# Key pass of a decoder's attention: transposes and scores of two units at a time, with eight places for turned keys

## The reference, cut to what matters

```python
# selected branch, per sequence b and kv head g (4 kv heads of 4 query heads, head size 128)
kg = gather_paged_rows(pool_k, page_table, new_k, kpos)        # raw rows of a paged cache
s  = einsum('btgrd,btgkd->btgrk', q, kg) * ATTN_SCALE
p  = masked_softmax(s, mask)
o  = einsum('btgrk,btgkd->btgrd', p, vg)
# window branch: the same over the last 512 rows (state_win_k, state_win_v)
```

## Time and profile before

| | |
|---|---|
| median of 3 executions | 3293.39 us (3290.66 to 3293.66) |
| the profiled execution | 3290.76 us, span 3288.9 us, mean granted clock 0.99 |
| TensorE busy | 3206.5 us, 97% of the span |
| VectorE (DVE) busy | 2032.2 us, 62% |
| ScalarE (ACT) busy | 1553.7 us, 47% |
| key pass | 1978.3 to 2147.9 us of the span |

### The profile page before, as it was taken

How to read it: one execution, slowest core, us unless ns; L and a number is a source line. 1 busy time by engine, 2 the same in 40 slices (tenths; PEclk the granted TensorE clock), 3 DMA queues, 4 the chain that set the end, 5 groups by cost and what they waited for, 6 DMA issues and landing times.

```text
span 3288.9 us, 69206 instructions
## 1 busy us (share of the span) xinstructions
PE 3206.5 (97%) x27708; PEld 3055.5 (93%) x27708; DVE 2032.2 (62%) x2281; ACT 1553.7 (47%) x1927; POOL 539.2 (16%) x477
## 2 busy tenths in 40 slices
PE   7999999999999999999999999999999999999998
PEld 6899889889999999999999997855999999999998
DVE  7999988865655544555665546455665554455566
ACT  4555555644544444444554433344554444444454
POOL 5666566620000000000000006000000000000000
PEclk9999999999999999999999999989999999999999
DMA  6445544456556555655556659889565655665553
GB/s 179 143 147 156 166 145 147 145 164 180 173 179 183 181 186 178 184 171 193 173 179 193 185 187 296 286 287 288 176 190 173 191 181 184 177 185 181 183 173 133
DMA packets 384392, 608.42 MB, mean 185 GB/s; under 512 B 52537, under 2 KB 144986, under 8 KB 383882
## 3 DMA queue, kind: packets, MB, share of 16 engines
q1 hardware_dynamic: 351738, 539.06, 52.7%
q10 hardware_dynamic: 29392, 60.86, 5.4%
q0 software_dynamic: 3024, 5.22, 0.4%
HBM read 594.83 MB, written 26.94 MB: 189 GB/s over the span
## 4 chain that ended last, share of the span: by engine, by line
PE 78%; DVE 14%; POOL 2%; issue 2%; ACT 2%; DMA 1%; SPq 0%; ACTq 0%; DVEq 0%; POOLq 0%
PE psum L407 22%; PE psum L408 22%; PE psum L409 22%; DVE rows_rest L1344 2%; PE psum L2322 2%; DVE turned L1403 2%; POOL prod_pool L1557 2%; PE psum L2332 1%; PE psum L1023 1%; PE psum L2370 1%; DVE normed_chunk L1428 1%; DVE turned L1394 1%; DVE state_ri L1411 1%; PE psum L1044 1%; PE psum L2220 1%
## 5 line engine op out<-in xcount | busy, mean ns | idle before, releaser
L390 DVE TENSOR_TENSOR w_rest<-w_raw,w_head 128x1024 fp32r<-128x1024 f32 x776 | 973.2, 1266 | 950.5 <-ACT w_head L386 949.7
L386 ACT ACTIVATE w_head<-w_raw 128x1024 fp32r<-128x1024 f32 x776 | 907.2, 1182 | 943.9 <-PE psum L409 906.4
L407 PE MATMUL psum<-act_head,w_head 128*128 128x264 f32 x4224 | 1204.5, 285 | 7.0 <-DVE act_rest L2757 5.8
L408 PE MATMUL psum<-act_rest,w_head 128*128 128x264 f32 x4224 | 1201.5, 284 | 0.0
L409 PE MATMUL psum<-act_head,w_rest 128*128 128x264 f32 x4224 | 1201.4, 284 | 0.0
L407 PEld LDWEIGHTS psum<-act_head,w_head 128*128 128x128 f32 x4224 | 824.5, 195 | 7.9 <-issue 6.0
L408 PEld LDWEIGHTS psum<-act_rest,w_head 128*128 128x128 f32 x4224 | 825.1, 195 | 0.2
L409 PEld LDWEIGHTS psum<-act_head,w_rest 128*128 128x128 f32 x4224 | 824.6, 195 | 0.0
L407 PE MATMUL psum<-hid_head,w_head 128*128 128x264 f32 x1408 | 400.0, 284 | 0.0
L408 PE MATMUL psum<-hid_rest,w_head 128*128 128x264 f32 x1408 | 399.9, 284 | 0.0
L409 PE MATMUL psum<-hid_head,w_rest 128*128 128x264 f32 x1408 | 399.9, 284 | 0.0
(11 more groups left out here) (421 smaller groups left out, 4092.3 us busy)
## 6 DMA issues: line engine op xcount, KB each, us to landing
w_raw<-in_ffn_w_gate SPq DMA_DIRECT2D x176, 512.0 KB, 4.3
w_raw<-in_ffn_w_up SPq DMA_DIRECT2D x176, 512.0 KB, 4.4
w_raw<-in_ffn_w_down SPq DMA_DIRECT2D x176, 512.0 KB, 3.7
w_raw<-in_cache_cmp_k SPq DMA_DIRECT2D x256, 128.0 KB, 2.6
w_raw<-in_cache_cmp_v SPq DMA_DIRECT2D x256, 128.0 KB, 2.6
w_raw<-in_ssm_w_glu SPq DMA_DIRECT2D x64, 512.0 KB, 4.1
w_raw<-in_ple_w_gate SPq DMA_DIRECT2D x64, 512.0 KB, 4.3
w_raw<-in_kv_w SPq DMA_DIRECT2D x48, 512.0 KB, 3.7
```

The source lines that it names most:

```text
L386: nc.scalar.activation(pairs(WH, u), tiles_of(RAW, u), ACT.Copy).then_inc(head_done, 1)
L390: nc.vector.tensor_tensor(pairs(WL, u), tiles_of(RAW, u), pairs(WH, u).bitcast(F32), ALU.subtract).then_inc(rest_done, 1)
L407: nc.tensor.matmul(o, wh, head, start=k == 0, stop=False)
L408: nc.tensor.matmul(o, wh, rest, start=False, stop=False)
```

## The change

TensorE's loop now goes by two units: it turns units u + 2 and u + 3, makes the scores of u and u + 1, and then does the side jobs of u and of u + 1. Before the loop units 0 and 1 are turned. The SBUF places for turned keys are eight instead of four (`KTS`, in three separate pieces of memory), and a copy waits for the scores of unit u - 4 instead of u - 2. The clearing of `QZ` is cut to the part that is read. The PSUM banks of the transposes, the wait of `turn_pe`, and the loops of DVE and ACT stay as they are.

```diff
     KT = sb("k_t", [P, 4, G * P])
     VO = sb("v_out", [P, 2, 4 * DH], at=kt_at)
+    KT3 = sb("k_t_third", [P, 3, G * P], at=wl_at + PAST * 4 + TS * P * 4)
+    assert wl_at + PAST * 4 + TS * P * 4 + 3 * G * P * 4 <= ph_at + 2 * T * 4
+    KT1 = sb("k_t_last", [P, G * P], at=pl_at)
+    KTS = [KT[:, k, :] for k in range(4)] + [KT3[:, k, :] for k in range(3)] + [KT1[:, :]]
...
-        V.memset(QZ[:, :], 0.0).then_inc(new_done, 1)
+        V.memset(QZ[:, 0:TS * P], 0.0).then_inc(new_done, 1)
...
-                                        KT[:, 2 * (u % 2) + e, g * P:(g + 1) * P], start=b == 0 and e == 0, stop=b == TS - 1,
+                                        KTS[2 * (u % 4) + e][:, g * P:(g + 1) * P], start=b == 0 and e == 0, stop=b == TS - 1,
...
-        if u >= 2:
-            eng.wait_ge(ks_done, 2 * (u - 2) + e + 1)
-        k = 2 * (u % 2) + e
+        if u >= 4:
+            eng.wait_ge(ks_done, 2 * (u - 4) + e + 1)
+        k, kt = 2 * (u % 2) + e, KTS[2 * (u % 4) + e]
         if e == 0:
-            nc.vector.tensor_copy(KT[:, k, :], PSUM[:, k, :]).then_inc(kt_taken[0], 1)
+            nc.vector.tensor_copy(kt, PSUM[:, k, :]).then_inc(kt_taken[0], 1)
         else:
-            nc.scalar.activation(KT[:, k, :], PSUM[:, k, :], ACT.Copy).then_inc(kt_taken[1], 1)
+            nc.scalar.activation(kt, PSUM[:, k, :], ACT.Copy).then_inc(kt_taken[1], 1)
...
         turn_pe(pe, 0)
-        for u in range(KSTEPS):
-            if u + 1 < KSTEPS:
-                turn_pe(pe, u + 1)
+        turn_pe(pe, 1)
+        for u in range(0, KSTEPS, 2):
+            for n in (u + 2, u + 3):
+                if n < KSTEPS:
+                    turn_pe(pe, n)
             scores_pe(pe, u)
+            scores_pe(pe, u + 1)
             beside_keys_pe(pe, u)
+            beside_keys_pe(pe, u + 1)
```

More of the change, by code:

```diff
@@ L132, in trunk_kernel @@
     ph_at = sb.at
+    ph_at = sb.at
     PH = sb("ple_head", [P, DEPTH, 2, T], F32R)
+    pl_at = sb.at
     pl_at = sb.at
```

## The result

The changed kernel takes 3325.47 us (median of 4 runs, 3324.93 to 3327.22), the kernel before 3292.02 (median of 4): ratio 1.0103, interval 1.0087 to 1.0119. It is slower by 1%. The profiled execution took 3327.22 us, 36.5 more than that of before. From its first scores to its last the key pass now lasts 201.9 us (1984.1 to 2186.0, from start to start), before 167.5 (1980.3 to 2147.8). With the first turns and the end of the last scores it is 206.5 us instead of 169.6. The stretches before and behind the pass moved by less than 2 us each.

What follows compares the result with a forecast made beforehand. TensorE's own instruction list was taken to bound the key pass. Waits for copies queued behind DVE's side jobs, less switches saved, sum to +29.0 us; clock +3.4 makes +32.4, from 3290.76 to 3323.2, given as 3325, range 3311 to 3350.

Steps and rivals of the forecast that it cites:

- Switches: TensorE's changes between turns and scores in the key pass: a pair of units saves 0.29 us, forty pairs 11.6 at most.
- Rope: Six pairs with a rope side job: TensorE waits 2.07 us for DVE's copy, round 6.75, +10.7 us in all.
- Rows: Twelve pairs with jobs of rows: TensorE waits 1.54 us for DVE's copies, less 0.29 saved, +15.0 us in all.
- the release: Step from the end of DVE's copy to TensorE's start, taken as 0.05 us.
- Second waits: Pairs where DVE's step u takes a group of scores or the maximum: 0.66 us more each, five times, +3.3.
- Window softmax: At u = 24, behind DVE's line held by POOL: TensorE waits 3.5 us more, against 2.27 before; net +0.9.
- Clock: Granted clock at 0.50 behind new waits: two of the six 2.07 us rope waits taken to lose it, +3.4 us.
- the early units: Units 0 to 11: waits and filling of 6.5 us, less 2.9 old and 1.7 saved, +1.9.
- the first, that only the switches count: Rival: key-pass side jobs add waits under 0.5 us each; 3279 us, or 3271 without old waits; chance 0.05.
- The second, the falling clock: Rival: clock stays down in rope pairs, 3351 us, with jobs of rows also 3391; chance 0.18.
- The third: Rival: eight places behind four PSUM banks let nothing run further ahead; savings and waits cancel, 3291 us; chance 0.03.
- the trace disagrees: Against the skill's rule that transposes don't count for the clock gate: the key pass held 1.00 over 2052 to 2095.

Runs made afterwards that it cites:

- experiment 1: Changed kernel with TensorE's old order (turn u + 1, scores u, side job u), eight places kept: 3293.06 us, ratio to the kernel before 1.0003.
- experiment 2: Changed kernel with DVE's and ACT's loops copying units u + 2 and u + 3 ahead of the pair's side jobs: 3281.28 us, second run 3282.14.
- experiment 4: Changed kernel with DVE's part of the twelve jobs of rows in its step u + 3 instead of u + 1: 3304.94 us.
- experiment 7: Changed kernel with DVE's copy of the rows made twice in each of the twelve jobs of rows: 3347.77 us, ratio to the kernel before 1.0165.
- experiment 8: Kernel before, in its old order, with DVE's copy of the rows made twice in each job of rows: 3292.08 us, ratio 0.9999.
- experiment 3: Kernel before (old order, four places), with DVE and ACT copying unit u + 1 before the side job of u: 3289.42 us, ratio 0.9988.
- experiment 5: Changed kernel with four places again, a copy waiting for the scores of u - 2; pair order kept: 3331.45 us, ratio to the kernel before 1.0114.
- experiment 6: Changed kernel with copies ahead of side jobs as in experiment 2, but four places as in experiment 5: 3293.45 us, ratio to the kernel before 1.0000.

## Why the prediction was right

3325.5 us was measured for 3325 predicted, slower as forecast. The mechanism was the one named, and experiments 1, 2, 4, 7 and 8 show it from both sides: move DVE's copies ahead of its side jobs and the wait goes, lengthen DVE's part and it grows, and in the old order of TensorE the longer part costs nothing. The signs came as named too: 30 waits for DVE's copy, 42.0 us (some 30 and 45 foretold), six of 2.01 and thirteen of 1.47. That the time hit so closely is in part luck: terms were off in both directions, and the pass took 206.5 us, where from 169.6 I had foretold about 200.

- *Switches.* 0.29 a pair predicted, 3.20 - 2.91 = 0.29 measured in plain pairs. Right, and shown by experiments 2 and 3.
- *Rope.* Wait 2.07 predicted, 2.01 listed; the round 6.88 instead of 6.75. *Rows.* 1.54 predicted, 1.47 listed; the round 5.01 instead of 4.88. Both rounds are 0.13 longer although the listed waits are shorter. One step that failed a little is the release: I took 0.05 us from DVE's end to TensorE's start, where the chain has 0.14; the other 0.04 stay open. The list counts a wait only from the last matmul's modelled end, so it hides some 0.2 in which the next could have started already; experiment 4 gives the true price of one, 5.01 - 3.34 = 1.67 us, where 1.47 is listed.
- *Second waits.* 0.66 predicted; rounds of 5.51 beside 5.01, so 0.5. In experiment 4 they did not show at all: they lengthen a wait more than they make one.
- *Window softmax.* 3.5 predicted, 3.3 listed.
- *Clock.* Two further stretches of 3.4 us at the lower clock predicted, three came (17 us against 6.8, 5 us lost). I had looked for them behind rope waits, and only one lies there, at 2041; the other two double the falls behind the long waits, of the gates and of the window softmax (6.6 and 6.7 us in the rows above, 3.4 each before). A second wait of 0.33 lies close behind the 2.01 at 2041; yet the same two, a round earlier, left the clock full. Why that rope wait and no other, the traces do not tell: up to the jobs of rows experiments 4 and 7 run the same program, and there it fell behind the first rope wait; in experiment 5, with the same rope waits, it fell behind none. So this term was a guess that came near, with its places wrong.
- *Sum.* +32.4 against +36.5 in the profiled executions. The 18 rounds with 0.13 each make some 2 us too little, the early units (7.3 us of waits listed, 6.5 predicted) and the clock (5 us, 3.4 predicted) some 3, an estimate; the second waits (5 x 0.16) and the softmax give back 1. The predicted 3325 was nearer because it allowed for the distance of the median from the profiled execution; the medians themselves are 33.5 apart.

The rivals: the first, that only the switches count, is what experiment 2 turned the kernel into, at 3281. Its condition, that no added wait stands behind a side job, was the right one, and it was not met. The second, the falling clock, did not decide here, but it was nearer than my 0.18 made it look: with 0.73 us more in a wait, experiment 7 lost it in eight of twelve rounds. The third has a true half: the places alone do nothing.

I had costed the eight places at nothing. For the changed kernel that holds within some 6 us (experiment 5); once the waits are gone they are worth 12 (experiments 2 and 6).

## What to carry to other kernels

Where one engine's list is batched in pairs, look up for each engine that feeds it what stands in that engine's list between the result it waits for and the last thing that it has handed over; an engine that is busy for less than half of the pass (DVE, 87 of 206 us) can still be late in every round. Batch the feeding engines' lists in the same change, ahead of the side jobs, and give the buffers for it. A small regular wait can cost little more than itself (1.47 us listed, 1.67 in the round), and with 0.73 us more cost twice as much (1.67 + 20.5 / 12 = 3.4 in experiment 7), because of the clock.

## What the runs showed of the hardware

- **Longer waits lost the clock more often, but no length decided alone.** Thirteen waits of 1.47 us, most of them one in each 5 us, left the granted clock at 1.00 over 2066 to 2140. With twelve waits of 2.20 us at the jobs of rows instead (experiment 7), the clock fell to 0.50 at eight. Of the six of 2.01 one lost it by itself, at 2041 (the fall at 2058 came in the 3.33 us wait right behind the sixth). Single waits went either way: behind one of 1.81 us in experiment 2 the clock fell (the line below), behind one of 2.15 in its second run and one of 2.41 in experiment 8 it stayed. So the prediction's ground for the waits of 1.54, the one of 1.8 that had left the clock full, was thinner than it looked. The Trainium skill (TensorE: Matmul & The Clock Gate, "HAM oscillation — how this bites in real kernels") has the mechanism, a gap in each round that sends the array back to 1.2 GHz. Its example has waits of 3 to 5 us for DMA; experiment 7 has 2.20 for a copy. A longer wait also leaves TensorE less busy in a round, and no run separates the two.

```profile
2001.97 3.54 PE L2328 MATMUL psum<-ident,tiles 128*128 128x128 f32 x16 [1.81 <-DMA tiles<-in_state_win_k]
```

- **Runs of sixteen transposes kept the full clock**, 1.00 over 100 us of experiment 2 (2020 to 2120). The Trainium skill (TensorE: Matmul & The Clock Gate, Part 4: PE-mode transpose) says that the full clock does not engage for transposes, which do not count as busy in the same way. In this mixture transposes do run at the full clock. Whether they count as work the trace can't tell, since scores and other matmuls lie between them; the prediction's "the trace disagrees" says more than it showed.
- **Going from turns (128x128) to scores (128x32, each in its own columns) and back costs 0.29 us a time, some 0.14 each way**: 3.20 us for two single units, 2.91 for a pair. The Trainium skill (TensorEngine Tiling (Array Packing), Key Properties) says that a change of tiling mode drains the engine. The trace is in line with it, for a turn behind full-width matmuls pays nothing of the kind (0.87 us against 1.02 behind scores); no run separates the mode from what else differs between turns and scores.
- **A DVE instruction on 128 numbers lasted until POOL's product ended.** In the changed kernel it again ended 0.02 us behind it, 2058.79 beside 2058.77; the next one of the same shape, with POOL's product done, took 0.16 us:

```profile
2056.43 2.34 POOL L2051 TENSOR_TENSOR q_t<-q_t,rope_part 128x1024 f32<-128x1024 f32 x1
2056.53 2.26 DVE L2573 TENSOR_TENSOR soft_rows<-soft_rows,gates_s 128x1 f32<-128x1 f32 x1
...
2058.82 0.16 DVE L2574 TENSOR_TENSOR soft_rows<-soft_rows 128x1 f32<-128x1 f32 x1
```

The Trainium skill (SBUF — State Buffer, "SBUF: two separate sides") says that a DVE instruction with two SBUF inputs and a GpSimd one hold a pair of ports in turn, each for its whole length. The trace agrees; no experiment here moved one of the two instructions to test it.
